# Two sums of weight quarters in the FFN block products, made by VectorE in place of GpSimd

## The reference, cut to what matters

```python
ffn = (jax.nn.silu(h @ w_ffn_gate[l]) * (h @ w_ffn_up[l])) @ w_ffn_down[l]
h = layer_norm(DEEPNORM_ALPHA * h + ffn, ln2_g[l], ln2_b[l])
```

## Time and profile before

| | |
|---|---|
| median of 3 runs | 724.86 us (724.34 to 725.07) |
| span of the profiled execution | 723.5 us |
| TensorE busy | 711.2 us, 98% of the span |
| VectorE busy | 510.2 us, 71% |
| ScalarE busy | 333.5 us, 46% |
| GpSimd busy | 135.9 us, 19% |
| the stage of the 18 units | 414.17 to 595.60 us |

### The profile page before, as it was taken

The page is one execution under the profiler, slowest core; times in us unless marked ns, Lnnn a source line. Parts: engine busy times, 40 slices in busy tenths (PEclk is TensorE's granted clock), DMA queues, the critical chain, the costliest instruction groups (busy, mean ns, idle before and its releaser), DMA issues.

```text
span 723.5 us, 11638 instructions
## 1 busy us (share of the span) xinstructions
PE 711.2 (98%) x4280; PEld 632.2 (87%) x4280; DVE 510.2 (71%) x883; ACT 333.5 (46%) x539; POOL 135.9 (19%) x167
## 2 busy tenths in 40 slices
PE   8999999999999999999999999999999999999995
PEld 7889888878888988888899899999999998888885
DVE  5323298797778785675889598999889885323577
ACT  6313576467777787322534244444444433312500
POOL 2516080512231220000000222222222200000001
PEclk9999999999999999999999999999999999999999
DMA  9425243112011205536622133233323334132102
GB/s 295 167 64 171 58 116 118 59 31 86 1 59 60 59 0 127 224 116 223 169 74 64 54 117 115 67 109 116 114 67 108 116 116 174 59 117 101 73 30 87
DMA packets 54756, 73.82 MB, mean 102 GB/s; under 512 B 4161, under 2 KB 40769, under 8 KB 54593
## 3 DMA queue, kind: packets, MB, share of 16 engines
q1 hardware_dynamic: 54432, 72.19, 30.7%
q0 software_dynamic: 144, 1.05, 0.7%
q10 hardware_dynamic: 144, 0.13, 0.1%
HBM read 70.21 MB, written 2.10 MB: 100 GB/s over the span
## 4 chain that ended last, share of the span: by engine, by line
PE 91%; DVE 5%; ACT 1%; issue 1%; DMA 0%; DVEq 0%; ACTq 0%
PE ps L1678 82%; PE ps L1690 3%; PE ps L1686 2%; PE ps L1687 2%; DVE wl L1100 1%; PE ps L1700 1%; DVE prob L1319 1%; ACT prob L899 1%; DVE ptl L1100 1%; PE ps L2087 0%; DMA arena<-in_x_t 0%; DVE vstat L1172 0%; DVE wl L1090 0%; DVE prob L1273 0%; PE ps L1830 0%
## 5 line engine op out<-in xcount | busy, mean ns | idle before, releaser
L1678 PE MATMUL ps<-wh,xh 128*128 128x512 f32 (+1 forms) x366 | 140.2, 383 | 0.1
L1678 PE MATMUL ps<-wh,xl 128*128 128x512 f32 (+1 forms) x366 | 139.4, 381 | 0.0
L1678 PE MATMUL ps<-wl,xh 128*128 128x512 f32 (+1 forms) x366 | 139.3, 381 | 0.0
L1678 PE MATMUL ps<-xh,wh 128*128 128x256 f32 (+1 forms) x416 | 135.0, 325 | 0.0
L1090 DVE TENSOR_TENSOR wl<-stage,wh 128x2048 fp32r<-128x2048 f32 (+1 forms) x28 | 63.7, 2275 | 98.9 <-ACT wh L713 64.4
L1678 PE MATMUL ps<-xh,wl 128*128 128x256 f32 (+1 forms) x416 | 131.7, 317 | 0.0
L1678 PE MATMUL ps<-xl,wh 128*128 128x256 f32 (+1 forms) x416 | 131.6, 316 | 0.0
L1678 PE MATMUL ps<-ath,wh 128*128 128x256 f32 (+1 forms) x280 | 86.1, 307 | 0.0
L1678 PE MATMUL ps<-ath,wl 128*128 128x256 f32 (+1 forms) x280 | 86.0, 307 | 0.0
L1678 PE MATMUL ps<-atl,wh 128*128 128x256 f32 (+1 forms) x280 | 86.0, 307 | 0.0
L1678 PEld LDWEIGHTS ps<-xh,wl 128*128 128x128 f32 x416 | 79.3, 191 | 5.4
(11 more groups left out here) (305 smaller groups left out, 1316.9 us busy)
## 6 DMA issues: line engine op xcount, KB each, us to landing
stage<-in_w_in SPq DMA_DIRECT2D x28, 512.0 KB, 4.6
stage<-in_w_ffn_gate SPq DMA_DIRECT2D x22, 512.0 KB, 4.7
stage<-in_w_ffn_up SPq DMA_DIRECT2D x22, 512.0 KB, 4.5
stage<-in_w_ffn_down SPq DMA_DIRECT2D x22, 512.0 KB, 3.7
stage<-in_w_out SPq DMA_DIRECT2D x8, 512.0 KB, 4.8
arena<-in_x_t SPq DMA_DIRECT2D x8, 256.0 KB, 5.2
stage<-in_w_in SPq DMA_DIRECT2D x8, 256.0 KB, 5.4
stage<-in_w_branch_nsa SPq DMA_DIRECT2D x4, 512.0 KB, 7.0
```

The source lines that it names most:

```text
L1678: return pe.matmul(out, (sh, sh, sl)[i], (mh, ml, mh)[i], start=start and i == 0, stop=stop and i == 2)
```

## The change

`mix_first` and `mix_third` are taken out of GpSimd's list and written into VectorE's. In `seven`, both stand right behind `sum_11`, ahead of `mix_second`. The wait of `mix_first` for `quad_lo` falls away (VectorE's own order gives it), its wait for the arrival of the load stays. `mix_third` no longer waits for `mix_s4`; it has a wait for `quad_lo` that VectorE itself has long fulfilled. The operations, their operands and shapes are as before.

```diff
@@ gpsimd
-            def mix_first(n, b, again=True):
-                pool.wait_ge(w_arrived[b], late_count(n + U_SEVEN, b))
-                if again:
-                    pool.wait_ge(quad_lo, 3 * n - 1)
-                pool.tensor_tensor(quads(mix, 0), raw_quads(b, K0, 1), raw_quads(b, K1, 1),
-                                   ALU.add).then_inc(mix_s1, 1)
-            def mix_third(n, b):
-                pool.wait_ge(mix_s4, n + 1)
-                pool.tensor_tensor(quads(mix, 3), raw_quads(b, K0, 0), raw_quads(b, K0, 1),
-                                   ALU.subtract).then_inc(mix_s3, 1)
...
-            pool.wait_ge(t_lo, 2)
-            mix_first(0, 0, False)
-            mix_third(0, 0)
-            mix_first(1, 1)
-            mix_third(1, 1)
-            with pool.Fori(1, N_SEVEN // 2) as j:
-                for b in range(2):
-                    mix_first(2 * j + b, b)
-                    mix_third(2 * j + b, b)
@@ vector
+            def mix_first(n, b):
+                dve.wait_ge(w_arrived[b], late_count(n + U_SEVEN, b))
+                dve.tensor_tensor(quads(mix, 0), raw_quads(b, K0, 1), raw_quads(b, K1, 1),
+                                  ALU.add).then_inc(mix_s1, 1)
+            def mix_third(n, b, again=True):
+                if again:
+                    dve.wait_ge(quad_lo, 3 * n)
+                dve.tensor_tensor(quads(mix, 3), raw_quads(b, K0, 0), raw_quads(b, K0, 1),
+                                  ALU.subtract).then_inc(mix_s3, 1)
...
             def seven(n, b, begin=False):
                 sum_11(n, b)
+                mix_first(n + 1, 1 - b)
+                mix_third(n + 1, 1 - b)
                 mix_second(n + 1, 1 - b)
                 raw_lo(n + 1, 1 - b)
...
+            dve.wait_ge(t_lo, 4)
+            mix_first(0, 0)
+            mix_third(0, 0, False)
             mix_second(0, 0)
             mix_fourth(0, 0)
             raw_lo(0, 0)
```

## The result

The changed kernel takes 729.7 us (median of 4 runs, 729.47 to 729.91), the kernel before 724.97 us beside it (4 runs). The ratio is 1.0065, 95% interval 1.0053 to 1.0077: slower by 0.65%. The span of the profiled execution is 728.1 us, against 723.5.

A forecast was written before the change was run, and what follows sets the result against it. TensorE bounds the stage until VectorE's lead is gone; 2.40 us a pair added less 1.80 returned, with the longer leg and restart, gives 5.1 us: 723.5 + 5.1 = 728.6 span, 730.0 median, range 726.5 to 733.5.

The forecast's parts named there:

- The bound and the lead: Stage of 18 units: TensorE never waits; VectorE, slower by 0.45 us a pair, hides behind a lead nearly used up.
- Cost of an added sum, 0.60: Each 128x512 sum added to VectorE's list costs 0.60 us, four a pair: 2.40 us.
- The return, 1.80 a pair: VectorE's `mix_lo` and `fact_of`, stretched under GpSimd's sums, get 1.80 us a pair back; 2.20 by the letter of the rule.
- The sum, 5.1 us: Net 0.60 us a pair over 8 pairs, longer leg to `raw_lo`, and restart: the stage ends 5.1 us later.
- The 0.1 for a restart: TensorE restarting behind a wait costs about 0.1 us: a matmul takes 0.47 where 0.40 is usual.
- Where it appears: Unit 1's `raw_lo` margin of 3.04 us shrinks 1.05 a pair, gone about unit 7; then TensorE follows VectorE.
- How it shows: In the stage's window TensorE's busy time falls some 5 us short, gaps at units' first matmul from about 7 on.
- The edits at nothing: Unit 0's sums, the load's wait and the last chores behind the stage cost nothing; the chores stay hidden by 0.3 us.
- The gaps are no reserve: VectorE's gaps of 0.85 and 0.57 us a pair end with ScalarE and move along, so added work isn't absorbed.
- The rival on the other side: The port gives back as much as the sums cost, 2.4 us a pair: 725.1 us, no measurable change; chance 0.11.
- The one with more than 0.60 a sum: Each added sum costs its whole duration or more: 7.9 us, 732.8; more than that, from waits in the loop, chance 0.14.
- the 0.22 us ahead of `sum_11`: Gap in VectorE's loop, offered as evidence that a wait released late is followed by some 0.2 us.

The follow-up runs named there:

- no_sums: Changed kernel with `mix_first` and `mix_third` made on neither engine except for unit 0, whose quarters later units use: 724.59 us, ratio 1.0001.
- early_first: Changed kernel with unit 1's `mix_first` made in an idle stretch of VectorE ahead of the stage: 729.06 us, ratio 1.0049.
- one_more: Changed kernel plus one more 128x512 sum a unit in VectorE's list, into a buffer nobody reads: 739.36 us, ratio 1.0208.
- swapped: Changed kernel with the two inserted sums the other way round, `mix_third` then `mix_first`: 731.68 us, ratio 1.0094.
- beside_read: Changed kernel with GpSimd again making two 128x512 sums a unit at the old times, into a buffer nobody reads: 746.15 us, ratio 1.0302.
- beside_write: Changed kernel with GpSimd doing a same-size memset behind a four-element sum, at each old sum's time: 730.14 us, ratio 1.0081.
- silu_later: Changed kernel with ScalarE's silu of an even unit's first sum put behind its rounding of the last quarters and block: 724.59 us, ratio 0.9999.

## Why the prediction was right, point by point

- **The bound and the lead.** Held. no_sums shows that TensorE is the bound. The lead is seen in the changed kernel's own rows: unit 1's `raw_lo` is there 3.1 us before TensorE starts it, units 0 to 7 are on time, and from unit 8 on TensorE follows. early_first shows that a longer lead puts that off.
- **Cost of an added sum, 0.60.** Held, by the rows (459.85, 460.45, 461.05) and by one_more's 1.20 a pair. It holds for a sum that the next instruction doesn't need, a condition that I hadn't put. That the order in the change met it was luck: with the other order the stage is 2.0 us longer (swapped).
- **The return, 1.80 a pair.** Held: 20.61 + 2.40 - 1.80 = 21.21 was forecast, 21.22 measured. beside_read shows that GpSimd's sums cause it and beside_write that it is their reading. The rule of the Trainium skill, SBUF — State Buffer, "SBUF: two separate sides", that of two such instructions the one that starts first holds the shared port for its whole length and the other fully blocks, is right in kind, and too high by 0.13 us a collision by these rows.
- **The sum, 5.1 us.** The stage grew by 5.09. `sum_11(16)` comes 169.30 us behind `sum_11(0)`, 4.82 more than the 164.48 of before; 4.80 was forecast. The 0.1 for a restart, read off a single row of another shape, was 0.10 here. In the profiled execution the span grew by 0.5 less, all of it ahead of the stage; that the 0.3 us between 730.0 and 729.7 is the same was not shown.
- **Where it appears.** At `raw_lo`, at a unit's first matmul, at a clock of 1.00: held. It begins at unit 8, one later than I said: the first pair took 20.92 us, 0.3 less than the others, and that much of the lead was left at unit 7.
- **How it shows.** Wrong in size: I expected TensorE's busy time to fall some 5 us short of the window, and it is 2.55 short. A matmul's row is 0.28 us long where the next starts after 0.12, so 0.16 us of each wait lies under the last row's tail, and the first row behind the wait is longer as well. The cost of the waits is in the starts (10.6 against 10.08 a unit), not in the idle column.
- **The edits at nothing.** Held. Unit 0's sums fit in ahead of the first `raw_lo`, which comes 9.1 us before the stage in both kernels and still has 1.87 us idle ahead of it, 2.11 before. At the end the bank was read 0.27 us before TensorE came for it, 0.3 by my working.
- **The gaps are no reserve.** Held for added work (one_more). Incomplete as a reading: the gap of 0.85 us was a matter of ScalarE's order, and was there to be had from that side (silu_later).

The rival on the other side failed at its own point: the return stayed at 1.8, not 2.4. The one with more than 0.60 a sum would have come near the time with the two sums swapped, but by the dependence and not by register work or waits. What I brought up for it, the 0.22 us ahead of `sum_11`, was no late release: the earlier trace rows name VectorE's own `fact_of` as the releaser.

## What to carry to other kernels

When the critical engine never waits, compare start-to-start paces, not busy shares: an engine that is slower by 2% can hide behind a lead for a whole stage, and any work added to it is paid in full once the lead is gone. Before moving an operation from GpSimd to VectorE, add up what its reads stretch on VectorE and set it against the cost of the operation there, and place it so that the next instruction doesn't read its result. A gap that ends with another engine may be closed from that engine's list, which here was worth as much as the whole move had cost.

## What the runs showed of the hardware

Three things that I hadn't expected to be so regular. VectorE's instruction with two SBUF inputs that starts under a reading GpSimd instruction is longer by the overlap less 0.12 to 0.15 us, in 108 of 108 cases, and a GpSimd memset that ran 0.37 us over one stretched it by nothing. A VectorE instruction that needs the result of the one just ahead, and waits for its semaphore, starts 0.12 us later than one that doesn't (0.72 against 0.60 for 128x512). And a matmul stream that stopped for some tenths of a microsecond pays 0.1 us to restart (0.22 us from the first start to the second, where 0.12 is usual), at a granted clock of 1.00 throughout.
